# Gate and up products of five feed-forward blocks in seven block products instead of eight, in one fp32 kernel

## Chip, cores and metric

The program runs on one core of a Trainium2 chip. The metric is device time of one execution in microseconds (us), the lower the better; a version's time is the median of its runs.

## What is computed

Two transformer blocks on one sequence of 512 tokens with 1024 features. The first adds 16 meta tokens (528 rows), runs two layers of feed-forward, mixer (pooling in layer 0, latent attention in layer 1), feed-forward, and normalises; the second runs an attention, convolution and gating mixer and one more feed-forward. The five feed-forward blocks (called f0 to f4 here) are what the change rewrites:

```python
def swiglu(h, w_gate, w_up, w_down):
    return (jax.nn.silu(h @ w_gate) * (h @ w_up)) @ w_down
# per layer: h = h + 0.5 * swiglu(rmsnorm(h, g), ...); D_MODEL 1024, D_FF 2816, fp32
# f0, f1: 528 tokens; f2, f3, f4: 512 tokens
```

## The kernel before

Activations lie transposed, features on the 128 partitions, tokens along a row. Each fp32 operand is split into a high half (fp32r, rounded) and a low half (the rest), and a product is three matmuls: high by high, high by low, low by high.

**Weights** come in units of 128 x 1024 numbers (512 KB). SyncE loads a unit into `raw`; ScalarE writes its high half `wH` (`split`, L1048) once TensorE has finished the unit four before; GpSimd writes the low half `wL` = raw - high (`lo`, L514); TensorE waits for it. `raw`, `wH`, `wL` have four slots each (`RING`). 425 units pass.

**A feed-forward** goes in two parts of 12 and 10 blocks of 128 hidden features (`PAIRS`). In a part, each iteration (a hardware loop) does two blocks: gate with two units, up with two units; a block is 8 k-steps x 3 matmuls over all tokens (512 columns, or twice 264). Over a feed-forward that is 11 iterations. VectorE scales gate by the norm (L1433), ScalarE applies silu (L1102), VectorE multiplies with up (L1440), ScalarE and VectorE make the halves `aH` and `aL` (L1106, L1445). Then the down products run in two groups of four output blocks; VectorE takes each from PSUM (L1458) and adds it to `h` (L1463). Matmuls are issued in `product` (L590). PSUM is four slots of two banks, taken in turn (`group`, `take`), so the slot that a new group takes is the one drained longest ago.

**Before a feed-forward** `prep` makes, as each row block k of `h` is ready, its square (ScalarE), the running sum of squares (VectorE, L1375), `xH` (ScalarE) and `xL` (VectorE, L1378). TensorE starts gate on `xH`, `xL` at once, and sums the squares over partitions (L608) after half of iteration 0 (`borrow`); the norm `rs` is applied behind the products.

**The second mixer** (near 1804 to 2015 us) runs attention heads, gate projections and a convolution of 31 taps; three channel blocks of taps are on VectorE (L1707), one on GpSimd (L527, L530).

The order of work is written out by hand, per engine, with semaphores.

Of the kernel before, what the change touches and what calls it, by code (L numbers as in the profile page):

```python
# [18 lines left out]
F32 = mybir.dt.float32  # L19
# [14 lines left out]
PAIRS = (6, 5)  # L34
FMAX = 2 * max(PAIRS)
NH, DN, DR, DV = 8, 64, 32, 64
# [11 lines left out]
RING = 4  # L48
# [11 lines left out]
TAB_Q, TAB_COS, TAB_SIN = range(3)  # L60


GAIN = {}
# [11 lines left out]
class Counts:  # L75
# [3 lines left out]
    def __init__(self):  # L79
        self.value, self.stride, self.slot, self.known = {}, {}, {}, False  # L80

    def start(self):
        self.n = {"pe": 0, "dve": 0, "act": 0}
        self.loop = {"pe": None, "dve": None, "act": None}

    def tick(self, eng, *names):
        self.n[eng] += 1
        for name in names:
            assert self.known or (eng, name) not in self.value, name
            self.value[eng, name] = self.n[eng]  # L90
            if self.loop[eng]:
                self.loop[eng][2].append(name)
# [5 lines left out]
    def at(self, eng, name, i=0):  # L98
        if not self.known:
            return 1  # L100
        v = self.value[eng, name]
        return v + self.stride[eng, name] * i if (eng, name) in self.stride else v

    def here(self, eng):

        lp = self.loop[eng]
        return self.n[eng] + (lp[0] * lp[1] if lp else 0)

    def enter(self, eng, key, i):
        stride = self.stride.get((eng, "loop:" + key), 1)  # L110
        self.loop[eng] = (i, stride, [], self.n[eng], key)

    def leave(self, eng, count):
        _, _, names, first, key = self.loop[eng]
        body = self.n[eng] - first
        self.stride[eng, "loop:" + key] = body
        for name in names:
            self.stride[eng, name] = body
            if eng != "pe":
                assert self.value[eng, name] - body == self.value[eng, name.replace(":L:", ":0:")]  # L120
        self.n[eng] = first + body * count
        self.loop[eng] = None


def units():

    out = []

    def ffn(f):
        for part, pairs in enumerate(PAIRS):  # L130
            for j in range(4 * pairs):
                out.append((f"gu{f}{part}", j))
            for j in range(2 * pairs):
                out.append((f"dn{f}{part}", j))

    def stage(name, n):
        out.extend((name, j) for j in range(n))

    ffn(0)
    stage("pool", 2)  # L140
    ffn(1)
    stage("dkv", 4)
    ffn(2)
    for name, n in (("dq", 3), ("uk", 1), ("uv", 1), ("uq", 4), ("wo", 4)):
        stage(name, n)
    ffn(3)
    for name, n in (("qk", 8), ("v", 4), ("cf", 8), ("sc", 12), ("br", 36), ("wo2", 8)):
        stage(name, n)
    ffn(4)
    return out  # L150


UNITS = units()
# [3 lines left out]
for _u, (_s, _j) in enumerate(UNITS):  # L157
    U0.setdefault(_s, _u)
# [9 lines left out]

RAW_AT = [16 * (u // RING + 1) for u in range(NUNITS)]


def first_order():

    order = [(k, "input") for k in range(4)]
    for k in range(0, 4, 2):
        order += [(k, "square"), (k + 1, "square"), (k + 4, "input"), (k + 5, "input")]
    return order + [(k, "square") for k in range(4, KD)]
# [35 lines left out]
def program(nc, w, out, C):  # L213
# [3 lines left out]
    with ctx:  # L217
# [23 lines left out]
        raw = place("raw", [P, RING, UW])  # L241
        wH = place("wH", [P, RING, UW], F32R)
        wL = place("wL", [P, RING, UW], F32R)
        h = place("h", [P, KD, T1])
# [16 lines left out]
        zx = zone(KD * T1 * 8)  # L261
        xH = place("xH", [P, KD, T1], F32R, zx)
        xL = place("xL", [P, KD, T1], F32R, zx + KD * T1 * 4)
        za = zone(FMAX * T1 * 8)
        aH = place("aH", [P, FMAX, T1], F32R, za)
        aL = place("aL", [P, FMAX, T1], F32R, za + FMAX * T1 * 4)
# [17 lines left out]
        kcat = place("kcat", [P, NH, T1], F32, zx)  # L284
        pT = place("pT", [P, 2, NT, SEQ], F32, zx + NH * T1 * 4)
# [4 lines left out]
        zc = za + 2 * CT * SEQ * 4  # L290
        zk = zc + 2 * CT * SEQ * 4
# [32 lines left out]
        zt = place("zt", [P, NT + 1, D], F32, za)  # L324
        bands = place("bands", [P, len(POOL_W), BAND], F32, zs)
# [88 lines left out]
        def _(sp):  # L414
# [14 lines left out]
            def load_ffn(f):  # L429
                gate, up, down = ffn_weights(f)  # L430
                row = 0
                for part, n in enumerate(PAIRS):
                    u = U0[f"gu{f}{part}"]


                    def gu(i, c, first=False):
                        for j in range(4):
                            if first and j in (1, 2):
                                load_x(4 * j - 4)
                                load_x(4 * j - 2)  # L440
                            elif first and j == 3:
                                sp.dma_start(cst[:, :], w["consts"]).then_inc(s_c, 16)
                            wt = (gate, gate, up, up)[j]
                            src = wt[(j % 2) * 4 * P:(j % 2 + 1) * 4 * P, bass.ds(c, 2 * P)]
                            load(u + j, src.rearrange("(a p) c -> p a c", p=P), i)

                    gu(0, row * P, f == part == 0)
                    with sp.Fori(1, n) as i:
                        gu(i, row * P + i * (2 * P))
                    u = U0[f"dn{f}{part}"]  # L450
                    for dg in range(2):
                        for j in range(n):
                            load(u + dg * n + j, kpart(down, row + 2 * j, 2, dg * BANK, (dg + 1) * BANK))
# [5 lines left out]
            for j in range(2):  # L459
                load(U0["pool"] + j,  # L460
                     w["pool_w"][0, 2 * j:2 * j + 2].rearrange("g (a p) d -> p (g a) d", p=P))
            load_ffn(1)
            sp.dma_start(tab[:, :, :], w["tables"]).then_inc(s_t, 16)
            for j in range(4):
                load(U0["dkv"] + j, kpart(w["w_dkv"], 2 * j, 2, 0, RKV + P))
            load_ffn(2)
            for j in range(3):
                load(U0["dq"] + j, kpart(w["w_dq"][0], 0, KD, j * P, (j + 1) * P))
            load(U0["uk"], kpart(w["w_uk"], 0, KKV, 0, NH * DN))
            load(U0["uv"], kpart(w["w_uv"], 0, KKV, 0, NH * DV))  # L470
            for j in range(4):
                load(U0["uq"] + j, kpart(w["w_uq"], 0, KQ, 2 * j * P, 2 * (j + 1) * P))
            for j in range(4):
                load(U0["wo"] + j, kpart(w["w_o"][0], 0, 4, 2 * j * P, 2 * (j + 1) * P))
            load_ffn(3)
            sp.wait_ge(dve_done, at("dve", "ol7"))
# [3 lines left out]
            def load_pair(u, c):  # L480
                for e in range(2):
                    load(u + e, kpart(win, 4 * e, 4, c, c + 2 * P))

            for e in range(4):
                load_pair(U0["qk"] + 2 * e, SEC["qk"[e // 2]] + 2 * (e % 2) * P)
            for j in range(4):
                load(U0["v"] + j, kpart(win, 2 * j, 2, SEC["v"], SEC["v"] + CW))
            for p in range(2):
                for e, s in enumerate(("cv", "cg")):
                    load_pair(U0["cf"] + 4 * p + 2 * e, SEC[s] + 2 * p * P)  # L490
            for p in range(2):
                for e, s in enumerate(("sx", "sc", "sb")):
                    load_pair(U0["sc"] + 6 * p + 2 * e, SEC[s] + 2 * p * P)
            for b, name in enumerate(("w_attn_out_2", "w_conf_out_2", "w_sc_out_2")):
                for p in range(4):
                    u = U0["br"] + (b * 4 + p) * 3
                    load_pair(u, SEC["gate"] + b * D + 2 * p * P)
                    load(u + 2, kpart(w[name][0], 0, CT, 2 * p * P, 2 * (p + 1) * P))
            for p in range(4):
                for e in range(2):  # L500
                    load(U0["wo2"] + 2 * p + e, kpart(w["w_o_2"][0], 4 * e, 4, 2 * p * P, 2 * (p + 1) * P))
# [8 lines left out]
        def _(pool):  # L510
            def lo(u, i=0):
                s = u % RING
                pool.wait_ge(h_done, u + 1 + RING * i)
                nc.gpsimd.tensor_tensor(wL[:, s, :], raw[:, s, :], f32(wH[:, s, :]),  # L514
# [1409 lines left out]
```

## Time and profile before

| | us |
|---|---|
| median of 3 runs (2642.26 to 2643.14) | 2642.27 |
| the profiled execution, device time | 2638.7 |
| its span, first to last instruction | 2636.9 |
| TensorE busy | 2587.6 (98%) |
| GpSimd / VectorE / ScalarE busy | 1136.5 / 966.0 / 863.3 |
| DMA engines, mean busy share of the main queue | 28.6% |

Matmuls are pipelined and their recorded durations overlap, so the pace of TensorE is to be read from the distance between starts (a stretch of the chain divided by its count), not from the mean duration.

### The profile page before, as it was taken

To read this page: it belongs to the slowest core of one execution; us is meant where nothing else is said; L and a number is where in the kernel's file an instruction comes from. 1 tells how busy PE (TensorE), PEld (TensorE's weight loads), DVE (VectorE), ACT (ScalarE), POOL (GpSimd) and SP (SyncE) were. 2 spreads that over 40 slices of the span, in tenths; PEclk is the share of its full clock that TensorE was granted. 3 is DMA by queue.
4 is the path that set the end of the run, shared out by engine and by line. 5 is a ranking of instruction groups with operands and counts; after the bars stand their busy time and mean duration, and the time that the engine had idled before them with its cause. 6 is when DMAs were issued, how large, how long until landed. Compare 5 with 4: busy or idle time off the path is not lost.

```text
span 2636.9 us, 35990 instructions
## 1 busy us (share of the span) xinstructions
PE 2587.6 (98%) x14302; PEld 2217.1 (84%) x14302; DVE 966.0 (37%) x1222; ACT 863.3 (33%) x1212; POOL 1136.5 (43%) x490
## 2 busy tenths in 40 slices
PE   8999999999999999999999999999889999999999
PEld 8999999999999888888678888867666888888887
DVE  5221226221226321225652212353996324422122
ACT  4222234221224321235642222334443423322221
POOL 4444433444435444444034344332877444444442
PEclk9999999999999999999999999999999999999999
DMA  5323332323323333323023233222112322332322
GB/s 167 90 87 90 94 98 65 88 88 91 93 90 89 105 95 90 95 87 96 17 72 95 88 101 93 95 80 64 48 41 64 95 92 93 96 96 87 99 94 72
DMA packets 197142, 229.45 MB, mean 87 GB/s; under 512 B 7072, under 2 KB 165408, under 8 KB 197040
## 3 DMA queue, kind: packets, MB, share of 16 engines
q1 hardware_dynamic: 197040, 227.99, 28.6%
q8 instruction: 76, 1.25, 0.2%
q14 instruction: 26, 0.21, 0.0%
HBM read 225.87 MB, written 2.10 MB: 86 GB/s over the span
## 4 chain that ended last, share of the span: by engine, by line
PE 90%; DVE 8%; issue 1%; ACT 1%; POOL 0%; DVEq 0%; POOLq 0%; ACTq 0%
PE ps L590 84%; DVE conv L1707 3%; PE ps L928 1%; PE ps L838 1%; DVE xL L1378 1%; PE ps L825 1%; PE ps L715 0%; DVE rl L1760 0%; PE ps L608 0%; PE ps L950 0%; PE ps L973 0%; DVE spls L1751 0%; PE ps L960 0%; PE ps L694 0%; PE ps L896 0%
## 5 line engine op out<-in xcount | busy, mean ns | idle before, releaser
L514 POOL TENSOR_TENSOR wL<-raw,wH 128x1024 fp32r<-128x1024 f32 x425 | 1036.3, 2442 | 1473.5 <-ACT wH L1048 1473.3
L1048 ACT ACTIVATE wH<-raw 128x1024 fp32r<-128x1024 f32 x425 | 446.8, 1058 | 1463.0 <-PE ps L590 1434.9
L590 PE MATMUL ps<-xH,wH 128*128 128x512 f32 (+1 forms) x2952 | 892.0, 342 | 10.8 <-DVE xL L1378 9.4
L590 PE MATMUL ps<-xL,wH 128*128 128x512 f32 (+1 forms) x2952 | 888.6, 341 | 0.0
L590 PE MATMUL ps<-xH,wL 128*128 128x512 f32 (+1 forms) x2952 | 886.5, 341 | 0.0
L590 PEld LDWEIGHTS ps<-xH,wH 128*128 128x128 f32 x2952 | 509.4, 189 | 86.3 <-POOL wL L514 11.1
L590 PEld LDWEIGHTS ps<-xL,wH 128*128 128x128 f32 x2952 | 506.7, 188 | 67.5 <-issue 3.1
L590 PEld LDWEIGHTS ps<-xH,wL 128*128 128x128 f32 x2952 | 508.7, 189 | 63.7
L590 PE MATMUL ps<-aL,wH 128*128 128x264 f32 (+1 forms) x1232 | 351.7, 332 | 0.0
L590 PE MATMUL ps<-aH,wL 128*128 128x264 f32 (+1 forms) x1232 | 351.5, 332 | 0.0
L590 PE MATMUL ps<-aH,wH 128*128 128x264 f32 (+1 forms) x1232 | 350.7, 331 | 0.0
L1440 DVE TENSOR_TENSOR m<-ps,t 128x512 f32<-128x512 f32 (+1 forms) x110 | 76.8, 698 | 518.3 <-PE ps L590 517.9
L590 PEld LDWEIGHTS ps<-aH,wH 128*128 128x128 f32 x1232 | 209.0, 188 | 24.2
L590 PEld LDWEIGHTS ps<-aH,wL 128*128 128x128 f32 x1232 | 208.8, 188 | 23.0
L590 PEld LDWEIGHTS ps<-aL,wH 128*128 128x128 f32 x1232 | 207.9, 188 | 23.3
L1458 DVE SCALAR_TENSOR_TENSOR m<-ps,rs 128x512 f32<-128x512 f32 (+1 forms) x80 | 55.8, 698 | 446.5 <-PE ps L590 445.6
L1433 DVE TENSOR_TENSOR t<-ps,rs 128x512 f32<-128x512 f32 (+1 forms) x110 | 76.3, 697 | 309.6 <-PE ps L590 309.5
L1445 DVE TENSOR_TENSOR aL<-m,aH 128x512 f32 (+3 forms) x110 | 165.8, 1546 | 49.8 <-ACT aH L1106 49.8
L1707 DVE SCALAR_TENSOR_TENSOR conv<-hb,gains,conv 128x512 f32<-128x512 f32 x90 | 100.7, 1119 | 3.0
L1102 ACT ACTIVATE t<-t 128x512 f32<-128x512 f32 (+1 forms) x110 | 63.5, 622 | 16.7 <-DVE t L1433 16.7
L1378 DVE SCALAR_TENSOR_TENSOR xL<-h,gains,xH 128x528 fp32r<-128x528 f32 (+1 forms) x64 | 61.4, 972 | 6.3 <-ACT xH L1067 4.1
L1106 ACT ACTIVATE aH<-m 128x512 f32 (+3 forms) x110 | 63.1, 621 | 0.0
(250 smaller groups left out, 1755.9 us busy)
## 6 DMA issues: line engine op xcount, KB each, us to landing
raw<-in_ffn_w_gate SPq DMA_DIRECT2D x88, 512.0 KB, 3.7
raw<-in_ffn_w_up SPq DMA_DIRECT2D x88, 512.0 KB, 3.7
raw<-in_ffn_w_down SPq DMA_DIRECT2D x88, 512.0 KB, 3.6
raw<-in_w_in SPq DMA_DIRECT2D x56, 512.0 KB, 3.5
raw<-in_w_ffn_in SPq DMA_DIRECT2D x44, 512.0 KB, 3.5
raw<-in_w_ffn_out SPq DMA_DIRECT2D x22, 512.0 KB, 3.6
raw<-in_w_o SPq DMA_DIRECT2D x12, 512.0 KB, 3.4
h<-in_tokens SPq DMA_DIRECT2D x4, 528.0 KB, 6.5
```

Of the source, the lines that this page charges most:

```text
L514: nc.gpsimd.tensor_tensor(wL[:, s, :], raw[:, s, :], f32(wH[:, s, :]), ALU.subtract).then_inc(l_done, 1)
L590: ins = nc.tensor.matmul(ps[:, 2 * s + c, 0:b - a], lhs, r[:, a:b], start=start and n == 0, stop=stop and n == 2, skip_group_check=True)
L825: ins = nc.tensor.matmul(b0[:, BANK - (i + 1) * P:BANK], q, kcat[:, hd, NMETA:NMETA + (i + 1) * P], start=True, stop=True)
L1048: nc.scalar.activation(wH[:, u % RING, :], raw[:, u % RING, :], ACT.Copy)\
L1102: fn(nc.scalar.activation(t2[:, j, 0:T], t1[:, j, 0:T], ACT.Silu), f"{st}:{it}:silu{j}")
L1106: fn(nc.scalar.activation(aH[:, bass.ds(2 * i + j, 1), 0:T] if it == "L" else aH[:, j:j + 1, 0:T], m[:, j:j + 1, 0:T], ACT.Copy), f"{st}:{ ...
L1378: do(V.scalar_tensor_tensor(xL[:, k, 0:T], src(p, k), gcol(*gain, k), f32(xH[:, k, 0:T]), ALU.mult, ALU.subtract), f"xl:{p}:{k}")
L1433: do(V.tensor_tensor(like(t1[:, j, 0:T], T), slot(name, T), like(norm(f), T), ALU.mult), "rd:" + name, f"{st}:{it}:g{j}")
L1440: do(V.tensor_tensor(like(m[:, j, 0:T], T), slot(name, T), like(t2[:, j, 0:T], T), ALU.mult), "rd:" + name)
L1445: do(V.tensor_tensor(aL[:, fl, 0:T], m[:, j:j + 1, 0:T], f32(aH[:, fl, 0:T]), ALU.subtract), f"{st}:{it}:lo{j}")
L1458: do(V.scalar_tensor_tensor(like(m[:, d % 2, 0:T], T), slot(name, T), 0.5 if f < 4 else 1.0, like(norm(f), T), ALU.mult, ALU.mult), "rd:" ...
L1707: do(V.scalar_tensor_tensor(conv[:, c, :], hb[:, c, tap:tap + SEQ], wt, conv[:, c, :], ALU.mult, ALU.add), name)
```

## The change

Gate and up of an iteration are a product of a 2 x 2 block matrix of weights (gate, up by the two halves of the 1024 inputs) with a 2 x 2 block matrix of activations (the two halves of the inputs by the two halves of the tokens). The change computes it with seven block products (Strassen, in Winograd's form) instead of eight. Each product is 4 k-steps x 2 feature blocks x 3 matmuls over half of the tokens (264 or 256 columns), and uses one weight unit: three units are loaded ones (products 1, 2, 4), four are sums of units (5, 6, 3, 7).

- **Weight sums** are made by VectorE into `wS` (L1593), their high half by ScalarE (L1154), their low half by VectorE (L1602). `wS` shares its memory with `wL`.
- **Low halves of plain units**, in the whole kernel: ScalarE writes -high into `wL` (L1158) and high into `wH` (L1159), and GpSimd issues a DMA that adds `raw` onto `wL` (L587).
- Slots: five for `wH`, `wL`; six for `raw`. A part is 6, 6, 6 and 4 hidden blocks.
- **Activation blocks**: seven blocks per input, in high and low halves. Differences and mixed blocks are made by VectorE (L1632, L1648, L1654, L1656) and split by ScalarE and VectorE. The sum of squares for f0, f1, f3, f4 moves to GpSimd (L599, L601).
- **PSUM**: products 1, 6, 7, 4 accumulate in slot x, 5 and 3 in y, 2 in z. ScalarE copies x after 1 (c1), y after 5 (c5) and x after 6 (c6) into `kept` before the next product goes on in that slot; VectorE reads x after 7 (u22, L1772) before product 4.
- Loops are written out.

```diff
-PAIRS = (6, 5)
+PAIRS = (3, 3, 3, 2)
-RING = 4
+RING = 5
+RAW = 6
+FIRST = (1, 5, 2, 6, 3, 7, 4)
+STEADY = (1, 5, 6, 3, 7, 2, 4)
+            parts = {1: {"raw": g1}, 2: {"raw": g2}, 4: {"raw": u2},
+                     5: {"add": (("raw", u1), ("raw", u2))},
+                     6: {"add": (("unit", at[5]), ("raw", g1))},
+                     3: {"add": (("unit", at[6]), ("raw", g2))},
+                     7: {"add": (("raw", u1), ("raw", g1))}}
...
-                nc.gpsimd.tensor_tensor(wL[:, s, :], raw[:, s, :], f32(wH[:, s, :]),
-                                        ALU.subtract).then_inc(l_done, 1)
+                    pool.wait_ge(n_done, ADDS[u])
+                    nc.gpsimd.dma_start(wL[:, u % RING, :], raw[:, UNITS[u].raw % RAW, :],
+                                        accum_op=ALU.add).then_inc(lo_in[u % RING], 16)
...
+                        x, y, z = (0, 3)[it % 2], 1, 2
+                        for i, p in enumerate(turns(part, it)):
+                            weights(u + i)
...
+                            elif p == 6:
+                                s = x
+                                pe.wait_ge(act_done, at("act", f"{st}:{it}:c1"))
+                            elif p == 3:
+                                s = y
+                                pe.wait_ge(act_done, at("act", f"{st}:{it}:c5"))
...
+                                if p == 4:
+                                    pe.wait_ge(dve_done, at("dve", f"{st}:{it}:u22{j}"))
...
+                            if first and i == 2:
...
+                                    borrow(f"f{f}", T, 3, SUMMED[f])
...
+                    order = (3, 1, 2, 0) if n % 2 else (0, 1, 2, 3)
...
+                                    sl.append(group(f"{st}:{4 * dg + d}", None, order[d]))
```

Three places of the order matter below.

VectorE, end of the first down part of f0, before: drains and adds (L1458, L1463), and then at once the next gate (L1433).

```order
L1458 SCALAR_TENSOR_TENSOR m<-ps,rs 128x528 [waits dve_done,pe_done]
L1463 TENSOR_TENSOR h<-h,m 128x528 [waits dve_done]
L1458 SCALAR_TENSOR_TENSOR m<-ps,rs 128x528 [waits dve_done,pe_done]
L1463 TENSOR_TENSOR h<-h,m 128x528 [waits dve_done]
L1433 TENSOR_TENSOR t_61<-ps,rs 128x528 [waits pe_done] x2
```

The same place now, with the second group of four output blocks whole:

```order
L1593 TENSOR_TENSOR wS<-wS,raw 128x1024 [waits raw_in3,dve_done,pe_done]
L1602 TENSOR_TENSOR wL<-wS,wH 128x1024 [waits hi_done]
L1822 SCALAR_TENSOR_TENSOR m<-ps,rs 128x528 [waits dve_done,pe_done]
L1827 TENSOR_TENSOR h<-h,m 128x528 [waits dve_done]
L1822 SCALAR_TENSOR_TENSOR m<-ps,rs 128x528 [waits dve_done,pe_done]
L1827 TENSOR_TENSOR h<-h,m 128x528 [waits dve_done]
L1822 SCALAR_TENSOR_TENSOR m<-ps,rs 128x528 [waits dve_done,pe_done]
L1827 TENSOR_TENSOR h<-h,m 128x528 [waits dve_done]
L1822 SCALAR_TENSOR_TENSOR m<-ps,rs 128x528 [waits dve_done,pe_done]
L1827 TENSOR_TENSOR h<-h,m 128x528 [waits dve_done]
L1593 TENSOR_TENSOR wS<-raw 128x1024 [waits raw_in0,raw_in1,pe_done]
```

A weight sum and a low half now stand ahead of the four drains; the last drain frees PSUM slot 0 (`order`), which is x of the next iteration 0.

ScalarE, start of f3, before: the last square and high half, and then the root of the norm.

```order
L1065 ACTIVATE sq<-h 128x512 [waits dve_done]
L1067 ACTIVATE xH<-h,gains 128x512
L1084 ACT_TABLE_LOAD
L1084 ACTIVATE sd<-var 128x512 [waits dve_done]
```

And now, from the last square to the copies c1 and c5:

```order
L1186 ACTIVATE sq<-h 128x512 [waits squares_done]
L1210 ACTIVATE xbH_71<-mix_256_93 128x256 [waits dve_done]
L1210 ACTIVATE xbH_71<-mix_256_94 128x256 [waits dve_done]
L1216 ACTIVATE xbH_71<-mix_256_93 128x2x256 [waits dve_done]
L1210 ACTIVATE xbH_71<-mix_256_93 128x256 [waits dve_done]
L1216 ACTIVATE xbH_71<-mix_256_94 128x2x256 [waits dve_done]
L1210 ACTIVATE xbH_71<-mix_256_94 128x256 [waits dve_done]
L1216 ACTIVATE xbH_71<-mix_256_93 128x2x256 [waits dve_done]
L1216 ACTIVATE xbH_71<-mix_256_94 128x2x256 [waits dve_done]
L1252 ACTIVATE kept<-ps 128x2x256 [waits pe_done]
L1154 ACTIVATE wH<-wS 128x1024 [waits dve_done,pe_done]
L1252 ACTIVATE kept<-ps 128x2x256 [waits pe_done]
```

All eight mixed blocks are split before c1 (the first L1252), for which product 6 waits.

VectorE, one middle iteration of f0 (there was a loop of seven instructions with their waits; L1788 and L1793 add gate parts, L1759 scales them, L1799 and L1733 multiply by silu, L1741 makes `aL`):

```order
L1593 TENSOR_TENSOR wS<-wS,raw 128x1024 [waits raw_in2,dve_done,pe_done]
L1602 TENSOR_TENSOR wL<-wS,wH 128x1024 [waits hi_done]
L1593 TENSOR_TENSOR wS<-wS,raw 128x1024 [waits raw_in5,dve_done,pe_done]
L1793 TENSOR_TENSOR t_62<-ps,kept 128x2x264 [waits act_done,pe_done]
L1759 TENSOR_TENSOR t_62<-t_62,rs 128x2x264 [waits dve_done]
L1602 TENSOR_TENSOR wL<-wS,wH 128x1024 [waits hi_done]
L1593 TENSOR_TENSOR wS<-raw 128x1024 [waits raw_in2,raw_in3,pe_done]
L1799 TENSOR_TENSOR m<-m,t_63 128x2x264 [waits dve_done,act_done]
L1602 TENSOR_TENSOR wL<-wS,wH 128x1024 [waits hi_done]
L1733 TENSOR_TENSOR m<-ps,t_63 128x2x264 [waits act_done,pe_done]
L1602 TENSOR_TENSOR wL<-wS,wH 128x1024 [waits hi_done]
L1741 TENSOR_TENSOR aL_70<-m,aH_69 128x1056 [waits act_done]
```

Eight instructions of 1024 numbers (four sums, four low halves) are new in each iteration.

## Rows read from the trace of the kernel before

**Rows 1.** The page: busy time of the engines; the DMA queue; issues to landing.

```profile
PE 2587.6 (98%) x14302; PEld 2217.1 (84%) x14302; DVE 966.0 (37%) x1222; ACT 863.3 (33%) x1212; POOL 1136.5 (43%) x490
...
q1 hardware_dynamic: 197040, 227.99, 28.6%
...
raw<-in_ffn_w_gate SPq DMA_DIRECT2D x88, 512.0 KB, 3.7
...
out<-h SPq DMA_DIRECT2D x8, 256.0 KB, 2.0
```

**Rows 2.** The chain in order of time: start us, us, engine and line.

```profile
24.13 375.06 PE ps L590 x3072
399.19 4.99 PE ps L715 x42
...
443.02 374.01 PE ps L590 x3072
...
848.37 11.14 PE ps L590 x48
859.55 356.49 PE ps L590 x1536
...
1358.65 347.88 PE ps L590 x1500
...
2276.79 356.23 PE ps L590 x1536
```

**Rows 3.** Groups by line and form: busy us, mean ns, idle before.

```profile
L514 POOL TENSOR_TENSOR wL<-raw,wH 128x1024 fp32r<-128x1024 f32 x425 | 1036.3, 2442 | 1473.5 <-ACT wH L1048 1473.3
...
L1048 ACT ACTIVATE wH<-raw 128x1024 fp32r<-128x1024 f32 x425 | 446.8, 1058 | 1463.0 <-PE ps L590 1434.9 <-PE ps L928 25.4 <-DMA raw<-in_ffn_w_gate 2.0
...
L1445 DVE TENSOR_TENSOR aL<-m,aH 128x512 f32 x54 | 79.8, 1516 | 24.4 <-ACT aH L1106 24.4
...
L1102 ACT ACTIVATE t<-t 128x512 f32<-128x512 f32 x66 | 37.7, 616 | 9.7 <-DVE t L1433 9.7
...
L1463 DVE TENSOR_TENSOR h<-h,m 128x512 f32<-128x512 f32 x48 | 33.2, 692 | 1.6
...
L1463 DVE TENSOR_TENSOR h<-h,m 128x528 f32<-128x528 f32 x32 | 22.7, 708 | 1.1
```

**Rows 4.** Timeline of VectorE at the end of f0: start us, us, instruction.

```profile
396.31 0.71 DVE L1458 SCALAR_TENSOR_TENSOR m<-ps,rs 128x528 f32<-128x528 f32 x1 [0.17 <-PE ps L590]
397.05 0.71 DVE L1463 TENSOR_TENSOR h<-h,m 128x528 f32<-128x528 f32 x1
397.67 0.70 DVE L1375 TENSOR_TENSOR ss<-ss,sq 128x528 f32<-128x528 f32 x1
```

**Rows 5.** Timeline at the start of f3, VectorE.

```profile
1348.07 0.69 DVE L1616 TENSOR_TENSOR h<-ps,h 128x512 f32<-128x512 f32 x1
...
1358.68 0.69 DVE L1398 TENSOR_SCALAR var<-ps 128x512 f32<-128x512 f32 x1 [5.95 <-PE ps L608]
1360.08 0.69 DVE L1405 TENSOR_TENSOR rs<-sd 128x512 f32<-128x512 f32 x1 [0.70 <-ACT sd L1084]
```

**Rows 6.** Timeline of the first microseconds, all engines.

```profile
6.30 2.35 POOL L514 TENSOR_TENSOR wL<-raw,wH 128x1024 fp32r<-128x1024 f32 x1 [5.87 <-ACT wH L1048]
6.46 2.70 ACT L1067 ACTIVATE xH<-h,gains 128x528 fp32r<-128x528 f32 x4 [0.24 <-DMA h<-in_tokens]
...
9.36 0.78 PE L590 MATMUL ps<-xH,wH 128*128 128x264 f32 x2 [9.36 <-DVE xL L1378]
```

**Rows 7.** Timeline of VectorE at the start of f2.

```profile
836.92 0.70 DVE L1498 TENSOR_TENSOR m<-ps,tab 64x528 f32<-64x528 f32 x1
```

**Rows 8.** The windows view, second mixer: engine busy sums (PE, DVE, ACT, POOL), clock, DMA share.

```profile
core 0: us, PE busy (x) PEld busy (x) DVE busy (x) ACT busy (x) POOL busy (x), PEclk, DMA share, GB/s
1804.00:2015.00 211.00, 188.02 (x786) 141.14 (x786) 170.03 (x205) 106.66 (x182) 149.07 (x80) 0.96 0.16 50
```

**Rows 9.** Convolution taps on VectorE, by source line: duration min/median/max in ns.

```profile
L1707 DVE SCALAR_TENSOR_TENSOR conv<-hb,gains,conv x90: 620/753/2783, 1844.7 to 1991.7; 128x512 f32<-128x512 f32 x90
```

More of the change, by code:

```diff
@@ L125, in units, with at, turns, __init__ @@
-def units():
-    out = []
+    def at(self, eng, name):
+        return self.value[eng, name] if self.known else 1
+    def here(self, eng):
+        return self.n[eng]
+FIRST = (1, 5, 2, 6, 3, 7, 4)
+STEADY = (1, 5, 6, 3, 7, 2, 4)
+XI = {4: 0, 7: 1, 6: 2, 2: 3, 3: 4, 5: 5, 1: 6}
+def turns(part, it):
+    return FIRST if part == it == 0 else STEADY
+class Unit:
+    def __init__(self, stage, j, raw=None, add=None):
+        self.stage, self.j, self.raw, self.add = stage, j, raw, add
+def units():
+    out, loads = [], []
+    def plain(name, n):
+        for j in range(n):
+            out.append(Unit(name, j, raw=len(loads)))
+            loads.append((name, j))
@@ L166, in tap_count, with landed, down_steps @@
     return 2 * tap + 1
[L169 to L177, printed above, removed]
+def landed(r):
+    return 16 * (r // RAW + 1)
+def down_steps(n, dg, part):
+    if dg and part == len(PAIRS) - 1:
+        return [(j,) for j in range(n - 2)] + [(n - 2, n - 1)]
+    return [(j,) for j in range(n)]
 def mla_order():
@@ L749, in _ @@
             ffn(1)
[L752 removed]
+            sl = [group(f"dkv:{d}", ("act", f"clat{d}") if d < KKV else None) for d in range(3)]
             for j in range(4):
@@ new lines, in sums @@
+            def sums(u, name=None):
+                if u >= NUNITS or UNITS[u].raw is not None:
+                    return
+                if name:
+                    on_pe(name)
+                a, b = UNITS[u].add
+                for what, i in (a, b):
+                    if what == "raw":
+                        dve.wait_ge(raw_in[i % RAW], landed(i))
+                    else:
+                        own(f"sum:{i}")
+                a, b = (raw[:, i % RAW, :] if what == "raw" else wS[:, i % RING, :] for what, i in (a, b))
+                do(V.tensor_tensor(wS[:, u % RING, :], a, b, ALU.add), f"sum:{u}")
@@ new lines, in ffn @@
+                    before = None
+                    for it in range(n):
+                        before = gating(f, part, it, before)
+                    up_first(f, before)
+                    hidden_low(f, before)
+                    last = part == len(PAIRS) - 1
+                    st = f"dn{f}{part}"
+                    for d in range(KD):
+                        name = f"{st}:{d}"
+                        dg = d // 4
+                        steps = down_steps(n, dg, part)
+                        if d % 4 == 0:
+                            for js in steps[:-1]:
+                                after(st, dg * n + js[0], f"{st}:u{dg * n + js[0]}")
```

966 lines of the change are left out of this document (626 added, 340 removed).

## Prediction

> **What bounds the kernel now.** The page comes first: TensorE is busy for 98% of the span, VectorE 37%, ScalarE 33%, GpSimd 43%, the DMA queue 28.6% [rows 1]. Then the chain in order of time: its long pieces are L590, 3072 matmuls in 375.06 and 374.01 us for f0 and f1 (122.1 and 121.8 ns each, 264 columns), 1536 in 356.49 and 356.23 us for f2 and f4 (232 ns each, 512 columns) [rows 2]. So inside a feed-forward nothing is waited for: TensorE's pace is the time, and the reader should see that fewer columns are fewer microseconds until a helper becomes late. The helpers' groups give their prices [rows 3]; the timelines give the starts of the feed-forwards, where they matter [rows 4 to 7].
>
> **A. Matmuls saved.** An iteration at 528 tokens had 4 units x 48 = 192 matmuls of 264 columns; it will have 7 units x 24 = 168. 24 x 0.122 = 2.93 us, for the 22 iterations of f0 and f1: 64.4. At 512 tokens, 96 x 0.232 = 22.28 us become 168 matmuls of 256 columns. Their pace is that of the 42 in 4.99 us [rows 2], 0.119: 19.99 us, 2.29 saved, x 33 = 75.6. **Sum -140.0.** Down products keep their matmuls.
>
> **Does an iteration hold its 20.5 (528) or 20.0 us (512)?** An SBUF operation of VectorE records 692 ns for 512 columns and 708 for 528 [rows 3], 1 ns a column, and the next starts 0.62 to 0.65 after it where nothing intervenes [rows 4]; I take 1.14 for 1024. Eight of those (sums, low halves) are 9.1, aL over 1056 about 1.2, six operations on 528 or 2 x 264 about 4.2, two on 264 0.7: 15 to 16 us, 75 to 79%. ScalarE, at 1.0 for a 1024-wide split (1058 recorded [rows 3]): seven highs and three negations 10, three copies and two silu at 0.6, aH 1.0: 14. Neither is full. The tightest point is c5: after product 1 ends ScalarE does c1, a negation, a high and sometimes aH, then c5, about 4.5 us, and product 3 wants it after 5.86. Slack 1.3 us. I cost the iterations at nothing; if that cover goes, each loses the shortfall (a rival below). Bound 0 to +27 (0.5 us each).
>
> **The adding DMAs.** 369 issues of 512 KB replace GpSimd's 2.44-us subtraction [rows 3]. No row shows one. Bounds per issue: GpSimd's 2.4 from below, which they replace, and from above a load's 3.7 from issue to landing [rows 1] twice over, 7.4, since the target is read too. I take 3.7. In gate and up 9 to 10 us lie between the negation and the need, in the rest one unit lasts 5.6 to 5.9 us and five slots (some 20 us) of lead. So both bounds are hidden: cost 0. The Trainium skill ("DMA: Bandwidth & Descriptors", Anatomy of one DMA — SWDGE (gpsimd) path) fits 2.0 us + bytes/436e3 for one DMA that GpSimd issues: an estimate of 3.2 us here; the sum would be the same.
>
> One row speaks against the change. L1445, VectorE with two SBUF operands while GpSimd subtracts, takes 1516 ns; L1463, the same shape where it mostly has the port alone, takes 692 [rows 3]. GpSimd is free of subtractions now, so I take 1.14, not 2.2 times as much, for the eight new operations. The Trainium skill ("SBUF — State Buffer", Who interferes with whom) says such a VectorE operation and a GpSimd instruction that reads SBUF lock each other out for a whole instruction; the row agrees. Were the issuing of adding DMAs to lock it likewise, VectorE would need an estimated 24 us in a 20-us iteration.
>
> **B. Starts of five feed-forwards.** Before, TensorE began on `xH`, `xL` and only the norm came later. Now product 6 waits for c1, which stands on ScalarE behind eight mixed blocks, and product 4 waits for u22, behind four sums, three low halves, the norm and the gate parts on VectorE. f3 in full. The stage before ends near 1346.6 (1358.65 [rows 2] less 48 matmuls, 11.1, and the statistics, about 1.0; its last drain is at 1348.07 [rows 5]); products 1 and 5, 48 block matmuls of 0.119, fill to 1352.4; product 2 starts when the second input half is there, ends 1355.3; statistics 1356.1. Mixed blocks: VectorE 1.4 and ScalarE 0.6 each in turn, half of them overlapped, 8 us from 1352.3 to 1360.3; c1 follows, product 6 starts at 1360.2 to 1360.8 (about 4 us idle) and 6, 3, 7 end at 1368.8. VectorE goes on from 1360.3 (its waits for ScalarE's halves are in the walk): sum 1.1, two lows 2.3, a gate part 0.6, sum 1.2, var 0.7, sd on ScalarE 0.7, three norm steps 2.2 (0.69 each, 0.7 idle before the second [rows 5]), gate 0.7, sum 1.1, gate part 0.6, gate 0.7, low 1.1, u22 0.7: done 1374.0. Product 4 ends 1377.0. Iteration 0 ended at 1358.65 + 48 x 0.232 = 1369.8 [rows 2]; with 2.29 saved 1367.5. Loss 9.5.
>
> The same walk for the others: f0 59.5 against 24.13 + 96 x 0.122 - 2.93 = 32.9, loss 26.6: xH of four blocks ends at 9.2 [rows 6], the eight squares of the sum are on GpSimd now (2.35 for 1024 columns [rows 6], so about 1.4 each for 528 with the wait) and end near 40.7, c1 behind them, matmuls start at half pace (0.78 for two at 9.36). f1 462.3 against 451.8: 10.5. f2 879.9 against 848.37 + 11.14 - 2.29 = 857.2: 22.7, because rotation (L1498 at 836.92 [rows 7]), latent norm and scales stand ahead of the mixed blocks. f4 2297.3 against 2276.79 + 11.14 - 2.3 = 2285.6: 11.7. **Sum +81.** Bounds: 40 (mixed blocks fully overlapped, one wait of the two gone) to 110 (GpSimd's squares slow VectorE down as in L1445).
>
> **C. Junctions.** A feed-forward has four parts, so three times a down part with all four drains in one go is followed by a new iteration 0 (15 in all). VectorE then does a sum and a low half (2.26) and four drains at 1.48 (two operations 0.74 apart [rows 4], 1.43 at 512); the last of them frees slot 0, which is x of product 1. From the last but one unit's end that is 7.6 us against TensorE's 5.86: +1.85 (6 times), at 512 7.45 against 5.57: +1.95 (9 times). **+28.7**, bounds 0 (the sum finished early) to 45 (the gate scale behind it late too).
>
> **D.** The last part drains its first four blocks late, and they stand behind sums at each stage's end: an estimate of half a microsecond each, **+2.5**.
>
> **E. Second mixer.** 1804 to 2015 us: VectorE 170 of 211 us, GpSimd 149 [rows 8]. Twenty units lose their subtraction: 49 us of GpSimd, and the 90 taps of 0.75 median, 2.78 longest [rows 9], meet it less; ScalarE gains 20 negations. Bounds -20 (half of what the taps take over the shortest, 0.62) and +10 (half of the negations on the path). I take **-8**.
>
> **Sum** -140.0 + 81 + 28.7 + 2.5 - 8 = -35.8, from the profiled 2638.7: 2602.9. The median of the runs stands 3.6 above the profiled execution, so 2606. A step of 0.2%, 5.3 us, is about what the measurement can tell from no change.
>
> **Rivals.**
> 1. *An iteration has no slack (slower).* c5 or c6 on ScalarE arrives late. Place: product 3 (product 6's copy before 7). It decides from 1.3 us more work ahead of c5, such as splits at 1.2 instead of 1.0 plus a late sum. At 1 us short in each of 55: 2606 + 55 = 2661. For: four engines chain in each product, VectorE at 79%. Against: each is under 80%. 0.12.
> 2. *The adding DMAs set the pace.* A load takes 1.7 us of the queue (512 KB at 228 MB in 0.286 x 2637 us), so a plain unit of 5.6 us holds until an add takes 3.9 us of queue time. At 5, some 180 plain units lose 1.0 and 55 iterations 1.6: +268, near 2870. The lock of L1445, if issuing caused it, would cost VectorE 8 x 1.3 us and so some 5 us in each iteration, of the same size. Against: a whole load lands in 3.7 us, latency included, so its share of the queue is less, and an add would have to cost more than twice a load. 0.10.
> 3. *Starts and junctions eat it all (no change).* Starts at 110, the rest as above: 2606 + 29 = 2635; junctions at 45 too: 2651. About 2642. 0.08.
> 4. *Starts are cheap.* Starts 40, junctions 14: 2606 - 41 - 14 = 2551. For: VectorE may interleave better than my serial walk. 0.10.
> 5. The change doesn't save the matmuls (pace of short ones is worse): against it the 42 in 4.99 us; no chance of its own.
>
> **Chances.** Forecast 0.60, its own range 2575 to 2637 (starts 60 to 105, junctions 15 to 45, mixer). Rivals 1 and 3 lie within the range to 2664, 2 and half of 4 outside it: 2555 to 2664. Faster: forecast and rival 4, 0.70. Within 0.2%: rival 3, 0.08. Slower: rivals 1 and 2, 0.22.
>
> **What the changed profile would show.** Right if: the chain has L590 pieces at 0.119 and 0.122 per matmul in steady iterations; TensorE idles once before product 6 and once before product 4 in each iteration 0, and some 1.9 us after each three-pair down part (releaser VectorE drain); VectorE's 1024-wide operations mean about 1.2 us; adding DMAs land within 4 us; the mixer stretch is a few microseconds shorter. Wrong if: TensorE idles before products 3 or 7 in middle iterations (rival 1), or waits on GpSimd's queue in projections and down parts (rival 2), or the sums take 2 us.

## The result and the profile after

The changed kernel takes 2659.78 us (median of 4 runs, 2655.59 to 2662.98), the kernel before 2642.70 on the same chip: ratio 1.0064, 95% interval 1.0046 to 1.0081. It is 17 us **slower**, where 36 us faster was forecast; of the range 2555 to 2664 the time lies near the upper end, on the other side of the kernel before. That it lies in the range at all is luck: the upper end was set by a rival (no slack in the iteration) that did not happen. The profiled execution spans 2661.2 us, 24.3 more than before.

The page of the kernel after: spans, busy times, the clock row, the DMA queues and the issues with their times to landing; they answer to [rows 1].

```profile
span 2661.2 us, 40041 instructions
...
PE 2479.1 (93%) x16150; PEld 2246.5 (84%) x16150; DVE 1567.9 (59%) x2096; ACT 1491.1 (56%) x1936; POOL 456.2 (17%) x462
...
PEclk7999998999999899999999999989999999999999
...
q0 software_dynamic: 53136, 193.49, 39.2%
q1 hardware_dynamic: 197040, 227.72, 26.5%
...
wL<-raw POOLq DMA_DIRECT2D x369, 512.0 KB, 5.7
raw<-in_ffn_w_gate SPq DMA_DIRECT2D x88, 512.0 KB, 5.9
```

TensorE has 108 us less to do and waits 133 us more: 93% busy where it was 98%. The mean granted clock is 0.968 (0.995 before). Where it waits, the view of waits of the kernel after says (engine and line, what released it, us in total, times, longest):

```profile
PEld ps L760 <- issue: 77.2, 23, 7.4
...
PE ps L760 <- DVE m L1822: 35.0, 15, 2.8
...
PE ps L760 <- DVE m L1772: 26.3, 5, 7.3
...
PEld ps L760 <- DVE xbL L1670: 21.8, 4, 7.7
...
PE ps L704 <- POOL ss L601: 18.9, 1, 18.9
...
PE ps L760 <- ACT kept L1252: 13.8, 2, 6.9
```

L1822 fifteen times is the junction of a down part with the next iteration 0; L1772 five times is u22 before product 4; L601 is the sum of squares of f0; L1252 is c1, ahead of product 6 in f3 and f4. The PEld rows are the weight loads' side of the same pauses, L1670 (halves of mixed blocks) that of product 6, and are not to be added. No row names a copy before product 3 or 7: in the steady iterations TensorE never waits. The last feed-forward in the chain in order of time (start us, us, engine and line; answers to [rows 2]):

```profile
2329.13 44.01 PE ps L760 x360
2373.14 32.97 PE ps L679 x144
...
2408.51 57.36 PE ps L760 x504
...
2501.25 57.36 PE ps L760 x504
...
2593.98 41.31 PE ps L760 x336
```

504 matmuls in 57.36 us are 0.1138 each, 19.12 us an iteration where it was 22.28. The last part, 336 in 41.31, is slower: 3.4 us of half clock at its start, and another pace, of which more at e0_same.

The helpers' groups of the kernel after, answering to [rows 3] (busy us, mean ns, idle before):

```profile
L587 POOL DMA_DIRECT2D wL<-raw x369 | 318.3, 863 | 2019.4 <-ACT wL L1158 1998.0
L1158 ACT ACTIVATE wL<-raw 128x1024 fp32r<-128x1024 f32 x369 | 389.7, 1056 | 328.7 <-PE ps L679 179.6
L1154 ACT ACTIVATE wH<-wS 128x1024 fp32r<-128x1024 f32 x220 | 233.5, 1061 | 568.0 <-DVE wS L1593 544.5
...
L1602 DVE TENSOR_TENSOR wL<-wS,wH 128x1024 fp32r<-128x1024 f32 x220 | 270.3, 1229 | 10.2 <-ACT wH L1154 9.2
L1593 DVE TENSOR_TENSOR wS<-raw 128x1024 f32<-128x1024 f32 x110 | 134.4, 1222 | 206.5 <-PE ps L760 195.8
```

A sum or a low half takes 1.22 to 1.23 us recorded, and the next one starts about 1.14 after, as taken.

### The profile page after: what moved, and what is told of

It reads as the page before. It is cut to its first block and busy times, and to the rows that moved or that the text cites. A ratio compares the mean times of both kernels' runs of the same rounds, so it can differ in the third digit from the quotient of the medians.

```text
span 2661.2 us, 40041 instructions
## 1 busy us (share of the span) xinstructions
PE 2479.1 (93%) x16150; PEld 2246.5 (84%) x16150; DVE 1567.9 (59%) x2096; ACT 1491.1 (56%) x1936; POOL 456.2 (17%) x462
## 3 DMA queue, kind: packets, MB, share of 16 engines
q0 software_dynamic: 53136, 193.49, 39.2%
## 5 line engine op out<-in xcount | busy, mean ns | idle before, releaser
L760 PE MATMUL ps<-xbH,wH 128*128 128x256 f32 (+1 forms) x3080 | 885.7, 288 | 109.4 <-DVE m L1822 35.0
L760 PE MATMUL ps<-xbL,wH 128*128 128x256 f32 (+1 forms) x3080 | 881.4, 286 | 0.0
L760 PE MATMUL ps<-xbH,wL 128*128 128x256 f32 (+1 forms) x3080 | 880.8, 286 | 0.0
L760 PEld LDWEIGHTS ps<-xbH,wH 128*128 128x128 f32 x3080 | 596.6, 194 | 119.7 <-issue 77.2
L587 POOL DMA_DIRECT2D wL<-raw x369 | 318.3, 863 | 2019.4 <-ACT wL L1158 1998.0
L760 PEld LDWEIGHTS ps<-xbL,wH 128*128 128x128 f32 x3080 | 595.8, 193 | 0.2
L760 PEld LDWEIGHTS ps<-xbH,wL 128*128 128x128 f32 x3080 | 595.7, 193 | 0.0
L1158 ACT ACTIVATE wL<-raw 128x1024 fp32r<-128x1024 f32 x369 | 389.7, 1056 | 328.7 <-PE ps L679 179.6
L1154 ACT ACTIVATE wH<-wS 128x1024 fp32r<-128x1024 f32 x220 | 233.5, 1061 | 568.0 <-DVE wS L1593 544.5
L1159 ACT ACTIVATE wH<-raw 128x1024 fp32r<-128x1024 f32 x370 | 387.2, 1046 | 2.0 <-DMA raw<-in_ffn_w_gate 2.0
L1602 DVE TENSOR_TENSOR wL<-wS,wH 128x1024 fp32r<-128x1024 f32 x220 | 270.3, 1229 | 10.2 <-ACT wH L1154 9.2
L1593 DVE TENSOR_TENSOR wS<-raw 128x1024 f32<-128x1024 f32 x110 | 134.4, 1222 | 206.5 <-PE ps L760 195.8
L679 PE MATMUL ps<-xH,wH 128*128 128x512 f32 (+1 forms) x488 | 191.2, 400 | 12.8 <-DVE m L1822 12.1
L1822 DVE SCALAR_TENSOR_TENSOR m<-ps,rs 128x512 f32<-128x512 f32 (+1 forms) x160 | 111.7, 698 | 151.7 <-PE ps L679 137.3
L1593 DVE TENSOR_TENSOR wS<-wS,raw 128x1024 f32<-128x1024 f32 x110 | 134.7, 1225 | 84.6 <-PE ps L679 79.8
L679 PE MATMUL ps<-xH,wL 128*128 128x512 f32 (+1 forms) x488 | 183.8, 385 | 0.0
```

The costliest lines, as they stand in the source:

```text
L587: nc.gpsimd.dma_start(wL[:, u % RING, :], raw[:, UNITS[u].raw % RAW, :], accum_op=ALU.add).then_inc(lo_in[u % RING], 16)
L679: ins = nc.tensor.matmul(ps[:, 2 * s + c, 0:b - a], lhs, r[:, a:b], start=start and n == 0, stop=stop and n == 2, skip_group_check=True)
L760: ins = nc.tensor.matmul(ps[:, 2 * s + j, 0:TH], lhs, rhs, start=p in (1, 5, 2) and k == q == 0, stop=p in (2, 3, 4) and k == KP - 1 and q ...
L1154: nc.scalar.activation(wH[:, s, :], wS[:, s, :], ACT.Copy).then_inc(h_done, 1)
L1158: nc.scalar.activation(wL[:, s, :], raw[:, r % RAW, :], ACT.Copy, scale=-1.0).then_inc(n_done, 1)
L1159: nc.scalar.activation(wH[:, s, :], raw[:, r % RAW, :], ACT.Copy).then_inc(h_done, 1)
```

## Where the 24.3 us come from

Stage by stage, from the first and last matmul of each in both traces. A start is what passes from the end of the stage before to the end of iteration 0, against the same before less one forecast iteration saving (2.93 or 2.29).

| term | forecast | profile |
|---|---|---|
| A matmuls saved | -140 | -149 (528 tokens: 22 x 2.83; 512: 9 iterations x 3.16, 24 x 2.41) |
| B starts | +81 | +129 (91 within iteration 0; 28 ahead of it; 9 of half clock behind the wait for u22, 11 in e0_same) |
| C junctions | +28.7 | +45 (idle 6 x 2.32 + 9 x 2.6 = 37.4, half clock behind five of them 7.5) |
| D late drains | +2.5 | +10 (one wait of 7.8 in f3 with 1.9 of half clock behind it, another mechanism) |
| E mixer, f3's end to f4's start | -8 | -5 (with a slot wait of 8.2 in it) |
| down products, 0.229 for 0.232 us | 0 | -6 |
| sum | -35.8 | +24 |

Start by start, B was forecast at 26.6, 10.5, 22.7, 9.5 and 11.7 us for f0 to f4, and the traces give 35, 22, 28, 25 and 19.

## Experiments

In each run's comparison the kernel before took 2641.4 to 2642.9 us; ratios are against it.

**e0_same: the changed kernel once more.** No edit.

> The changed kernel once more, unedited, to see what of its profile repeats. Theory: the idle times of TensorE (15 of 2.4 to 2.8 us after down parts, starts of f0 to f4, 8 us at 1722 and 8.4 at 1749) come back at the same places within 0.3 us, and the time is 2656 to 2663. Open: whether the pace of the block matmuls at 512 tokens (0.113 us in some parts, 0.118 in others) falls in the same parts again. If it belongs to the program, it does; if it is a state in which the chip happens to be, the parts differ, and the total moves by up to 0.8 us for each iteration that changes.

Measured: 2661.05 us (2654.5 to 2667.6), ratio 1.0065 (1.0041 to 1.0090). The same waits stand at the same places, 15 of 2.4 to 3.2 us before product 1 among them; two are 1 us longer, more than expected (20.0 for 18.9 in f0, 8.3 for 7.3 before product 4 of f2). The chain of f4 reads:

```profile
2409.74 57.36 PE ps L760 x504
...
2502.48 59.60 PE ps L760 x504
...
2597.46 39.81 PE ps L760 x336
```

The second part, 57.36 us in the first profile, takes 59.60 here, with no wait and no half clock in either; the third, 41.31 there, 39.81 here. Block matmuls at 512 tokens start 0.113 us apart in some parts and 0.118 in others, throughout a part, and which parts differs between two executions of one program. Nine iterations ran at the faster pace in the first profile and six here, 2.2 us in all. The runs spread by 0.5% where those of the kernel before spread by 0.1%; how much of that is the pace is not shown, since only one execution of each run has a profile. What chooses the level is open; edits below are read from stages of the profile as well as from medians.

**e1_slots: product 1 takes the slot drained first.**

```diff
-                        x, y, z = (0, 3)[it % 2], 1, 2
+                        x, y, z = (3, 0)[(part + it) % 2], 1, 2
...
-                                    borrow(f"f{f}", T, 3, SUMMED[f])
+                                    borrow(f"f{f}", T, 0, SUMMED[f])
...
-                    order = (3, 1, 2, 0) if n % 2 else (0, 1, 2, 3)
+                    order = (0, 1, 2, 3) if x == 3 else (3, 1, 2, 0)
```

> The slot that VectorE drains last is no longer the slot of the next part's product 1; all 15 junctions are touched. Theory (slot reuse causes the stall): the 15 idle times of 2.4 to 2.8 us are gone, and with them some clock drops: 35 to 42 us less, near 2620. Rival (VectorE is simply late there: the sum and low half ahead of the drains make the next weights or copies late too): the idle time moves to product 5 or 6 of iteration 0, and less than 15 us are gained.

Measured: 2623.07 us, ratio 0.9934 (0.9913 to 0.9954). One place suffices to read it. VectorE at the first junction of f0, timeline, first the changed kernel, where TensorE's product 1 starts at 147.24 (2.43 after its last down matmul):

```profile
139.26 1.23 DVE L1593 TENSOR_TENSOR wS<-wS,raw 128x1024 f32<-128x1024 f32 x1 [3.43 <-PE ps L679]
140.40 1.22 DVE L1602 TENSOR_TENSOR wL<-wS,wH 128x1024 fp32r<-128x1024 f32 x1
141.72 0.71 DVE L1822 SCALAR_TENSOR_TENSOR m<-ps,rs 128x528 f32<-128x528 f32 x1
...
146.39 0.71 DVE L1822 SCALAR_TENSOR_TENSOR m<-ps,rs 128x528 f32<-128x528 f32 x1
```

and then e1_slots, where product 1 starts at 143.34, without a gap:

```profile
138.81 1.22 DVE L1602 TENSOR_TENSOR wL<-wS,wH 128x1024 fp32r<-128x1024 f32 x1
140.14 0.71 DVE L1822 SCALAR_TENSOR_TENSOR m<-ps,rs 128x528 f32<-128x528 f32 x1
...
144.80 0.71 DVE L1822 SCALAR_TENSOR_TENSOR m<-ps,rs 128x528 f32<-128x528 f32 x1
```

The drains are as late as ever; only nobody waits for the last. The 15 waits are gone, the span is 40 us shorter, and the change is faster than the kernel before. Half a microsecond comes back before product 6 at each of the nine junctions of 512 tokens, where c1 is late now, and two iterations have the faster pace, not nine (5 us). With both, the edit is worth 45 to 50 us, where the table has 45: the junction term is shown, half clock included.

**e2_turn: the turn of slots after a feed-forward.** The changed kernel gives feed-forwards fixed slots, and the count by which later stages take slots no longer points at the one drained first.

```diff
+                count[0] = -(-count[0] // SLOTS) * SLOTS
```

> After each feed-forward the turn of slots starts at the slot drained first; nothing else changes. Theory (the turn is out of step, so the next stage asks first for a slot drained late): idle times at the ends of f1 (3.5 us), f2 (1.3) and f3 (8.4) shrink to about 0, 1 and 2: 8 to 11 us less. Rival (the preparation of the next input, 3.6 us of VectorE work per output block, is what is late): the same idle times remain with another releaser, under 3 us gained.

Measured: 2660.96 us, ratio 1.0065 (1.0047 to 1.0083): nothing in sum. By stages both are half right. f1 to f2 takes 24.9 us (28.6 and 29.8 in the two profiles of the changed kernel), f3's end to f4's start 537.7 (545.0, 541.7); but f2's end to f3's start 153.0 (147.3, 144.5). A turn right for one stage is wrong for the attention behind f2. The waits after f1 (3.5 us) and f3 (8.4) were slot waits. But an earlier start is not all gain: in f2 product 4 now comes 37.2 us after the first block matmul (34.9 before the edit), so of 3.7 us some 1.4 remain; in f3, which starts 5.7 later, it comes after 32.0 and not 35.6. VectorE's walk sets product 4, whenever TensorE begins.

**e3_heads: a small load goes behind the weights.**

```diff
-            sp.wait_ge(dve_done, at("dve", f"up:gu3{len(PAIRS) - 1}:{PAIRS[-1] - 1}"))
-            sp.dma_start(heads[0:2 * NH, :], w["heads"]).then_inc(s_h, 16)
...
             for e in range(4):
                 load_pair(SEC["qk"[e // 2]] + 2 * (e % 2) * P)
+            sp.wait_ge(dve_done, at("dve", f"up:gu3{len(PAIRS) - 1}:{PAIRS[-1] - 1}"))
+            sp.dma_start(heads[0:2 * NH, :], w["heads"]).then_inc(s_h, 16)
```

ScalarE at the end of f3 in the changed kernel, timeline, shows the wait:

```profile
1716.86 0.61 ACT L1257 ACTIVATE t<-t 128x512 f32<-128x512 f32 x1
1726.51 1.06 ACT L1158 ACTIVATE wL<-raw 128x1024 fp32r<-128x1024 f32 x1 [9.03 <-DMA raw<-in_w_in]
1727.47 1.04 ACT L1159 ACTIVATE wH<-raw 128x1024 fp32r<-128x1024 f32 x1
1728.42 1.04 ACT L1287 ACTIVATE aH<-m 128x1024 fp32r<-128x1024 f32 x1
```

`aH` was ready to be made at 1718.5, but a split of a mixer unit stands ahead of it, whose load was issued only at 1717.4, behind `heads`.

> The small load of heads, which waits for VectorE's last product of f3, goes into SyncE's queue behind the eight mixer units and no longer ahead of them. Theory (the weights queued behind it are late, and ScalarE waits for them with the high half of the hidden values behind it): the 8.0 us idle of TensorE before the last down products of f3 go, and the 8.4 behind shrink in part: 8 to 14 us less. Rival (raw slots come free late because of the adding DMAs, 5.7 us to landing): the units are still late, under 2 us gained.

Measured: 2656.36 us, ratio 1.0059 (1.0042 to 1.0075). The 8.0 us wait is gone, f3 takes 368.1 us (377.4, 378.9). The 8.4 behind it stays: that one is the slot turn. The median moved by 3.4 us, less than the stage and within the spread; the gain is read from the stage alone.

**e4_squares: f0's squares between the mixed blocks.**

```diff
-                for what, k in MIXED:
+                for i, (what, k) in enumerate(MIXED):
+                    if f == 0:
+                        square(0, i)
                     (block6 if what == 6 else block47)(f, k)
...
-            for k in range(KD):
-                square(0, k)
```

> In f0 alone ScalarE writes the eight squares one by one between the eight mixed blocks, and no longer all of them behind. Theory (product 6 of f0 waits 19 us because c1 stands on ScalarE behind eight squares that GpSimd takes at 1.4 us each): the idle time before the statistics falls from 19 to 20 us to under 6, f0 ends 11 to 15 us earlier, the rest as before. Rival (the mixed blocks on VectorE set it, GpSimd's sums are hidden in them): under 3 us.

Measured: 2656.21 us, ratio 1.0052 (1.0036 to 1.0069); f0 takes 393.4 us (400.2, 399.5). Half of the forecast: the wait before the statistics falls from 18.9 to 12.1 us, not under 6. GpSimd's sums still end only at 39.2 us (46.3 before the edit): by the timeline, with two buffers for squares, ScalarE and GpSimd take turns and ScalarE waits three times 2.4 to 2.5 us for VectorE's mixed blocks in between.

**e5_pool_lows: the subtraction back on GpSimd.**

```diff
-                    pool.wait_ge(n_done, ADDS[u])
-                    nc.gpsimd.dma_start(wL[:, u % RING, :], raw[:, UNITS[u].raw % RAW, :],
-                                        accum_op=ALU.add).then_inc(lo_in[u % RING], 16)
+                    pool.wait_ge(h_done, u + 1)
+                    nc.gpsimd.tensor_tensor(wL[:, u % RING, :], raw[:, UNITS[u].raw % RAW, :], f32(wH[:, u % RING, :]),
+                                            ALU.subtract).then_inc(lo_in[u % RING], 16)
```

> Low halves of plain units by GpSimd's subtraction again, without the negation on ScalarE and without adding DMAs. Theory (adding DMAs cost nothing and the subtraction disturbs VectorE): VectorE's sums and low halves go from 1.22 us to 1.4 to 2.5 in the mean, product starts in iterations get late, and the time is 10 to 60 us over the changed kernel. Rival (the adding DMAs and negations are a cost of the change: loads land after 5.9 us and not 3.7): 5 to 20 us faster than the changed kernel.

Measured: 2698.62 us, ratio 1.0218 (1.0201 to 1.0235), 38 over the changed kernel. Groups of VectorE in e5_pool_lows (busy us, mean ns):

```profile
L1591 DVE TENSOR_TENSOR wS<-raw 128x1024 f32<-128x1024 f32 x110 | 172.6, 1569 | 175.0 <-PE ps L760 170.4 <-DMA raw<-in_ffn_w_up 3.3 <-DMA raw<-in_w_ffn_in 1.2
L1739 DVE TENSOR_TENSOR aL<-m,aH 128x1024 fp32r<-128x1024 f32 (+1 forms) x55 | 144.3, 2623 | 34.0 <-ACT aH L1285 31.0
```

Of VectorE's three kinds of sums and low halves only this one is slower in the mean (1.57 us for 1.22), beside `aL` (2.62 for 1.24) and some smaller operations. Only those that meet a subtraction are: of the 110 sums, 35 overlap one and take 2.32 us, the other 75 take 1.22. f3's end to f4's start takes 562.2 us (545.0, 541.7): of the 38 us half are the mixer's. So the adding DMAs, with the negations that they need on ScalarE, are a gain of this change over the subtraction, not its cost. The run does not separate the two.

**e6_warm: TensorE kept busy while it waits for the mixed blocks.** In f2 the added matmuls overwrite half of the latent statistics, so its latent norm is changed.

```diff
+                                if T == SEQ:
+                                    for _ in range(32 if f == 2 else 56):
+                                        nc.tensor.matmul(ps[:, 7, 0:TH], bH[:, XI[1], 0, 0:P],
+                                                         bH[:, XI[1], 1, :], start=True, stop=True,
+                                                         skip_group_check=True)
```

> Adds matmuls of 128 by 256 into an unused PSUM bank behind the statistics of f2 (32), f3 and f4 (56 each), where TensorE idles 5 to 7.5 us; their result is not used. Theory (idle time is followed by a stretch at half clock that costs another 2 to 3 us at each start): the granted clock stays 1.0 there, iteration 0 of f3 and f4 is 2 to 3 us shorter, in all 4 to 9 us less. Rival (the walk of VectorE to u22 sets product 4, and the half clock lies inside that wait): products 6, 3, 7 are faster, the wait before product 4 grows by the same, 0 to 2 us gained.

Measured: 2660.86 us, ratio 1.0084 (1.0067 to 1.0101). The stretch from f4's statistics to the wait for u22, windows view (us, PE busy, clock, DMA share, GB/s), in the changed kernel and then in e6_warm:

```profile
2306.00:2324.00 18.00, 11.31 (x72) 0.72 0.50 118
```

```profile
2296.00:2313.00 17.00, 15.37 (x124) 1.00 0.49 119
```

The clock is 1.0 and not 0.72, products 6, 3 and 7 end earlier, and the wait for u22 grows from 5.1 to 5.9 us. From f4's first block matmul to product 4 it is 35.07 us, as it was (35.09); f3 35.63 (35.64). The rival holds: VectorE's walk sets product 4, and the half clock ahead of it costs nothing.

**e7_norm_later: norm and gate scales behind u22.**

```diff
-                            if first and i == 2:
+                            if first and i == 5:
...
-                    if p == 6 and first:
+                    if p == 7 and first:
                         if f == 2:
...
                             scales(f"f{f}", T)
                         gate(0)
+                        gate(1)
```

> In iteration 0 of each feed-forward VectorE computes the scales of the norm, and scales the gate, behind u22 and no longer ahead of it; the statistics go behind product 7 on TensorE, the root behind c6 on ScalarE. Nothing else changes, against the changed kernel at 2660. Theory (product 4 waits because the norm's walk on VectorE stands ahead of u22): the five waits before product 4 (4.3, 5.0, 7.3, 5.0, 5.2 us) fall under 1.5 us each, the half clock behind them (11 us together) goes too, and the wait for GpSimd's sum in f0 shrinks: 28 to 45 us less, 2615 to 2632. Rival (the work is only later: silu, the next copies and iteration 1 wait in place of product 4): idle times of the same sum inside iteration 1, under 10 us gained.

Measured: 2651.54 us (9 runs), ratio 1.0033 (1.0019 to 1.0047). The five waits before product 4 are gone, but in the waits of e7_norm_later stands

```profile
PE ps L760 <- DVE wL L1602: 14.4, 7, 5.1
```

Five of the seven are in iteration 1 (1.3 to 5.1 us each), where low halves are behind the moved norm. Iteration 0 of the five feed-forwards is 37 us shorter in all, iteration 1 is 16 us longer: the theory and the rival each have about half. The feed-forwards are 2.5 to 6.5 us shorter (f4 not, which has the slower pace throughout here), and the gain is 8 us by median and 17 by span.

**best and best2: the edits together.** `best` is e1, e3, e4, and e2's line for f1 and f3 alone; `best2` is that with e7.

> All four edits together, the turn of slots only after f1 and f3: slots of junctions, heads load behind, squares between the mixed blocks. Theory: the gains add, 38 (slots) + 8 (heads) + 12 (squares) + 5 to 9 (turn) from 2660: 2590 to 2600, faster than the kernel before by 1.6 to 2.0%. Rival (part of it was given back elsewhere): 2605 to 2615.

> The same edit on top of the four edits that gave 2606. Theory: the two gains are independent, 2562 to 2580, 2.3 to 3.0% under the kernel before. Rival: mixed blocks, half clock and the walk overlap, so that only 5 to 15 us remain: 2590 to 2600.

Measured: 2606.39 us, ratio 0.9870 (0.9854 to 0.9886); and 2585.77 us, ratio 0.9790 (0.9767 to 0.9813). `best` falls where its rival put it, not its theory; `best2` lies between its two, 21 us under `best`. Seven block products do pay: 2.1% under the kernel before (1.9 to 2.3), 74 us under the change as made. What remains is in the page of best2:

```profile
span 2586.3 us, 40041 instructions
...
PE 2458.6 (95%) x16150; PEld 2229.6 (86%) x16150; DVE 1572.6 (61%) x2096; ACT 1484.0 (57%) x1936; POOL 455.4 (18%) x462
```

## Why the prediction was wrong

**The step that failed is the size of B, the starts**, and behind it C. The mechanisms were named (product 6 behind c1, product 4 behind u22, the slot drained last), the places too; 81 was the forecast of B, 110 its upper bound, and 129 is the measured sum. Three things were missing.

*The second input half was late.* For f3 I let TensorE go on as the last drains came: second half there 5.7 us after the first block matmul, product 4 after 27.4. VectorE's timeline of the changed kernel:

```profile
1368.43 1.22 DVE L1593 TENSOR_TENSOR wS<-wS,raw 128x1024 f32<-128x1024 f32 x1
1369.56 1.22 DVE L1602 TENSOR_TENSOR wL<-wS,wH 128x1024 fp32r<-128x1024 f32 x1
...
1374.97 1.54 DVE L1593 TENSOR_TENSOR wS<-wS,raw 128x1024 f32<-128x1024 f32 x1
1376.43 1.21 DVE L1602 TENSOR_TENSOR wL<-wS,wH 128x1024 fp32r<-128x1024 f32 x1
...
1381.13 1.40 DVE L1648 SCALAR_TENSOR_TENSOR mix<-d5s,gains,u12s 128x256 f32<-128x256 f32 x1
...
1389.85 1.29 DVE L1670 SCALAR_TENSOR_TENSOR xbL<-mix,xbH 128x512 fp32r<-128x512 f32 x2
...
1406.62 0.75 DVE L1772 TENSOR_TENSOR m<-ps,kept 128x256 f32<-128x256 f32 x2
```

Block matmuls start at 1371.65. Two sums and two low halves, 4.9 us, stand among the drains of the stage before, so mixed blocks begin 9.5 us after the start, not 5.7, take 9.9 and not 8, and the walk behind them 16.2, not 13.7: product 4 at 35.6. This is read from the timeline; no run moved these sums. In f0 it is GpSimd that is later than I had it:

```profile
37.77 8.52 POOL L601 TENSOR_TENSOR ss<-ss,sq 128x528 f32<-128x528 f32 x6 [0.75 <-ACT sq L1186]
```

The sums end at 46.3 us, not near 40.7: they begin only at 32.7, behind the mixed blocks, and the first takes 4.3 us (the last six 1.42 each, as taken). e4_squares gains 6.8 us there.

*Work ahead of the start.* I counted only iteration 0. The stages before f1, f2 and f3 grew by 11.2, 10.2 and 5.3 us. Of f2's, 3.5 are the slot turn, which e2_turn shows (most of it would be waited for again before product 4); for the rest the traces show differences and first blocks on VectorE behind the last drain and half clock, and no run tells these apart.

*The clock.* I gave it a word in f0 alone. TensorE is busy for 121 us of the half-clock stretches in the changed kernel and for 20 in the one before; half of that, 60 and 10 us, is an estimate of what they cost its matmuls. Where VectorE sets the next wait that is free (e6_warm); behind waits for u22 and junctions it is not: 9 to 11 and 7.5 us.

**A** was mis-sized by 9 in the other direction: I took the pace of short matmuls of another kind, 0.119, and they run at 0.113 or 0.118. **C**: my 1.85 and 1.95 us are 2.32 and 2.6, with half clock behind a third of them. The terms that I named give 1.74 and 1.88 (7.6 less 5.86, 7.45 less 5.57), and drains stand 1.56 us apart there (three from 141.72 to 146.39), not 1.48. **D**: late drains cost little, but a load in SyncE's queue, passed over because the diff does not touch it, is late now and cost 8, with 2 of half clock behind it; the slot turn, also untouched, another 8 (in E's stretch). **E** was right in sign; e5_pool_lows shows that the adding DMAs are worth some 17 to 20 us in that stretch.

**No slack in the iteration, and adding DMAs setting the pace**, the two slower rivals, did not happen: no wait before 3 or 7, none on GpSimd's queue. An adding DMA lands after 5.7 us where I took 3.7, a load after 5.9 (3.7 before), and both are hidden. By the fit in the Trainium skill ("DMA: Bandwidth & Descriptors", Anatomy of one DMA — SWDGE (gpsimd) path) the estimate for one DMA was 3.2 us; the measurement, 369 of them beside the loads, is 5.7, and it decides. L1445's 1516 ns were contention with a subtraction, and an issue of 0.86 us does not cause it: VectorE's 1024-wide operations hold 1.22 us beside 369 of them. The outcome is what the third rival described, starts and junctions eating the saving; and 18 us beyond its 2642, 9 beyond its upper case of 2651. I gave it 0.08: its upper bounds were taken for rare, though nothing in the rows held them down.

## What to carry to other kernels

A saving inside a steady loop is easily forecast from pace times count; what it costs at each entry must be walked through with all that stands on the helper's queue there, the weight work for later units included, and with the half clock behind every new wait. When a rotation of buffers is replaced by fixed places, look at who takes the one drained last, in the next stage too. Fifteen waits of 2.4 to 3.2 us went with four edited lines.

## What was not expected of the hardware

- One program, two paces: 256-column matmuls at a granted clock of 1.0 start 0.113 or 0.118 us apart for a whole part, in other parts in another execution (57.36 or 59.60 us for 504). Matmuls of 264 columns stay at 0.122. Its cause was not found.
- Down products of 512 columns start 0.229 us apart in the kernel after, 0.232 in the one before (144 of them take 33.1 us to the end of the last, 288 take 67.1). The same question stands there.
- DMA engines at 0.85 mean share in a steady part (2410 to 2428 us, 205 GB/s) and TensorE waits for none of them.
